# Queries split in two halves, and score buffers handed back by their readers' own signals, in the sparse attention of a decoder step

## The reference

```
o_c, p_c = _sdpa(qb, kc, vc, dist_c, dist_c >= 0, slopes_a)      # 32 compressed keys
...
o_s, _ = _sdpa(qb[:, :, None], kg, vg, dist_s, dist_s >= 0, slopes_a)   # selected blocks: all 16 of 16 here
...
o_w = _window_banded(qn, kw[:, w_buf:], vw[:, w_buf:], slopes_a)        # the last 512 keys
...
o_a = g[..., 0, :] * o_cs[..., 0, :] + g[..., 1, :] * o_cs[..., 1, :] + g[..., 2, :] * o_w
```

## Time and profile before

| | |
|---|---|
| device time, median of 3 runs | 2226.22 us (2226.08 to 2226.61) |
| the profiled execution: its time, its span | 2227.57 us, 2225.8 us |
| mean granted TensorE clock | 0.955 |
| the sparse attention | 715.8 to 1024.0 us of the span |
| TensorE busy in it | 287.48 us of 308.20 us |
| VectorE, ScalarE busy in it | 216.52 us, 177.07 us |
| ScalarE's operations for `qhi` in it | 8 of 1.02 us |
| VectorE's subtractions for `qlo` in it | 8 of 1.23 us |

### The profile page before, as it was taken

How to read it: one execution, slowest core, us unless ns; L and a number is a source line. 1 busy time by engine, 2 the same in 40 slices (tenths; PEclk the granted TensorE clock), 3 DMA queues, 4 the chain that set the end, 5 groups by cost and what they waited for, 6 DMA issues and landing times. The chain is left out here.

```text
span 2225.8 us, 34082 instructions
## 1 busy us (share of the span) xinstructions
PE 2040.4 (92%) x12618; PEld 1822.0 (82%) x12618; DVE 1140.2 (51%) x2499; ACT 621.7 (28%) x1204; POOL 114.6 (5%) x174
## 2 busy tenths in 40 slices
PE   6989999998995999998888969699999999999997
PEld 1338889878995888887667957499999999999996
DVE  0434333332234677776786644455555555555555
ACT  2113333321223565655771012211101111111012
POOL 1021100001300000000120000000000000000000
PEclk9989998999996999998998989899999999999998
DMA  9765544321101000000003431221111111101104
GB/s 318 259 190 177 158 142 147 107 79 49 49 1 62 1 2 1 1 1 1 1 0 117 148 141 40 67 79 36 57 37 48 57 28 57 57 28 57 38 0 153
DMA packets 132539, 166.42 MB, mean 75 GB/s; under 512 B 15852, under 2 KB 98636, under 8 KB 132373
## 3 DMA queue, kind: packets, MB, share of 16 engines
q1 hardware_dynamic: 117790, 134.75, 19.0%
q0 software_dynamic: 4832, 17.15, 2.4%
q10 hardware_dynamic: 9808, 13.11, 1.7%
HBM read 144.31 MB, written 22.77 MB: 75 GB/s over the span
## 5 line engine op out<-in xcount | busy, mean ns | idle before, releaser
L1673 DVE TENSOR_TENSOR late_x<-late_x,ffn_po 128x344 f32<-128x344 f32 x528 | 244.3, 509 | 116.3 <-PE ffn_po L1603 116.1
L1586 PE MATMUL ffn_pg<-late_words_hi,ffn_uhi 128*128 128x344 f32 x528 | 169.3, 321 | 14.8 <-DVE ffn_ulo L1637 14.8
L1547 ACT ACTIVATE ffn_sg<-ffn_pg 128x344 f32<-128x344 f32 x66 | 30.2, 458 | 534.2 <-PE ffn_pg L1586 534.2
L1603 PE MATMUL ffn_po<-ffn_a_hi,ffn_ohi 128*128 128x344 f32 x528 | 169.0, 320 | 0.2 <-DVE late_x L1673 0.2
L1586 PE MATMUL ffn_pg<-late_words_lo,ffn_uhi 128*128 128x344 f32 x528 | 169.1, 320 | 0.0
L1586 PE MATMUL ffn_pg<-late_words_hi,ffn_ulo 128*128 128x344 f32 x528 | 169.1, 320 | 0.0
L1603 PE MATMUL ffn_po<-ffn_a_hi,ffn_olo 128*128 128x344 f32 x528 | 168.9, 320 | 0.0
L1586 PE MATMUL ffn_pv<-late_words_hi,ffn_uhi 128*128 128x344 f32 x528 | 168.8, 320 | 0.0
L1586 PE MATMUL ffn_pv<-late_words_lo,ffn_uhi 128*128 128x344 f32 x528 | 168.7, 319 | 0.0
L1586 PE MATMUL ffn_pv<-late_words_hi,ffn_ulo 128*128 128x344 f32 x528 | 168.7, 319 | 0.0
L1603 PE MATMUL ffn_po<-ffn_a_lo,ffn_ohi 128*128 128x344 f32 x528 | 168.2, 319 | 0.0
(11 more groups left out here) (465 smaller groups left out, 4654.0 us busy)
## 6 DMA issues: line engine op xcount, KB each, us to landing
mod_wr<-in_w_ada SPq DMA_DIRECT2D x12, 2048.0 KB, 8.8
ffn_raw_u<-in_w_ffn_in SPq DMA_DIRECT2D x44, 512.0 KB, 5.8
kin_kin<-in_cache_kv SPq DMA_DIRECT2D x64, 256.0 KB, 3.5
ffn_raw_o<-in_w_ffn_out SPq DMA_DIRECT2D x22, 512.0 KB, 3.5
gate_d<-dec_gate ACTq DMA_DIRECT2D x48, 172.0 KB, 2.9
late_x<-gate_d SPq DMA_DIRECT2D x8, 1032.0 KB, 5.3
dec_raw<-in_w_in POOLq DMA_DIRECT2D x16, 512.0 KB, 5.6
dec_vin<-in_cache_kv SPq DMA_DIRECT2D x64, 128.0 KB, 2.1
```

Source lines behind the costliest of these rows:

```text
L1547: act.activation(sg[(j + c) % 2][:], pg[(j + c) % 2][:, 0:TCH], ACT.Silu).then_inc(silu_done, 1)
L1586: mm = pe.matmul(bank[b][:, 0:TCH], w[j][:, v * KD + k, :], h[:, k, tok], start=(k == 0 and q == 0), stop=(k == KD - 1 and q == 2))
L1603: mm = pe.matmul(po[u % 4][:, 0:TCH], w[j][:, k * P:(k + 1) * P], a[j][:, tok], start=(q == 0), stop=(q == 2))
L1673: dve.tensor_tensor(total[:, k, tok], total[:, k, tok], po[u % 4][:, 0:TCH], ALU.add).then_inc(o_read, 1)
```

## The change

First, ScalarE and VectorE treat the queries in two halves of 512 columns each: `qhi` is made by two operations, each with an increment of `q_hi`, and `qlo` by two, each of which waits for its half. The second operation on VectorE may begin when the second on ScalarE is done. TensorE needs both halves (`q_lo`, new) before it scores with them or overwrites the buffer.

Second, `sc_free` goes. TensorE waits, by the kind of item n - 2 (the new function `drained`), for the semaphore which the operation that reads that buffer increments itself: `q_lo`, `c_in` (new), `c_ev`, `c_add` or `biased`. With it VectorE's wait for its own operation and the separate increment go, 144 times in all: 16 units, "turned" and "blocks" in each of 8 heads. One wait is new on VectorE: `biased`, ahead of the operations that halve the slope tables at the start of heads 1 to 7.

```diff
--- before.py
+++ after.py
@@ -615,8 +615,8 @@
         if at == Q_AT and h + 1 < NH:
             items.append(("queries", h + 1))
         items.append(("unit", u))
-    place = {x: n for n, x in enumerate(items)}
     scored = np.cumsum([kind != "queries" for kind, x in items]).tolist()
+    HALF = SEQ // 2
     groups = [(x[5] - x[4] + 511) // 512 for x in units]
     turned_up_to = np.cumsum([0] + groups).tolist()
     second = np.cumsum([0] + [n - 1 for n in groups]).tolist()
@@ -638,7 +638,7 @@
         tp = [s.ps(f"tp{i}", [P, 512]) for i in range(2)]
         out = [s.ps(f"out{i}", [P, 2, P]) for i in range(2)]
         q_dup, q_ps, q_hi = s.sem("q_dup"), s.sem("q_ps"), s.sem("q_hi")
-        sc_full, sc_free = s.sem("sc_full"), s.sem("sc_free")
+        sc_full, q_lo, c_in = s.sem("sc_full"), s.sem("q_lo"), s.sem("c_in")
         tab, biased, p_full = s.sem("tab"), s.sem("biased"), s.sem("p_full")
         tp_full, tp_act, tp_dve = s.sem("tp_full"), s.sem("tp_act"), s.sem("tp_dve")
         pv_done, o_free, shares, o_step = s.sem("pv_done"), s.sem("o_free"), s.sem("shares"), s.sem("o_step")
@@ -699,17 +699,30 @@
                                            g.z[:, k0 // P + q, VCOL[b]:VCOL[b] + P], start=(q == 0), stop=(q == nt - 1))
                     mm.then_inc(pv_done, 1)
 
+                def drained(kind, x):
+
+                    if kind == "queries":
+                        pe.wait_ge(q_lo, 2 * x + 2)
+                    if kind == "compressed":
+                        pe.wait_ge(c_in, x + 1)
+                    if kind == "turned":
+                        pe.wait_ge(c_ev, x + 1)
+                    if kind == "blocks":
+                        pe.wait_ge(c_add, x + 1)
+                    if kind == "unit":
+                        pe.wait_ge(biased, x + 1)
+
                 for n, (kind, x) in enumerate(items):
                     slot = n % 2
                     if n >= 2:
-                        pe.wait_ge(sc_free, n - 1)
+                        drained(*items[n - 2])
                     if kind == "queries":
                         pe.wait_ge(q_dup, 2 * x + 2)
                         for t in range(TT):
                             mm = pe.transpose(sc[slot][:, t * P:(t + 1) * P], qd[:, t].rearrange("p a b -> p (a b)"), g.ident[:])
                         mm.then_inc(q_ps, 1)
                     if kind == "compressed":
-                        pe.wait_ge(sc_free, place["queries", x] + 1)
+                        pe.wait_ge(q_lo, 2 * x + 2)
                         for i in range(TT):
                             mm = score(slot, 32 * i, x, i, 0, 32, g.kkc)
                         mm.then_inc(sc_full, 1)
@@ -752,7 +765,8 @@
                 for n, (kind, x) in enumerate(items):
                     if kind == "queries":
                         act.wait_ge(q_ps, x + 1)
-                        act.activation(qhi[x % 2][:], sc[n % 2][:], ACT.Copy).then_inc(q_hi, 1)
+                        for a in range(0, SEQ, HALF):
+                            act.activation(qhi[x % 2][:, a:a + HALF], sc[n % 2][:, a:a + HALF], ACT.Copy).then_inc(q_hi, 1)
                     if kind == "unit":
                         h, k, i, b, k0, k1 = units[x]
                         if x >= LAG:
@@ -821,27 +835,27 @@
                 for n, (kind, x) in enumerate(items):
                     at_sc = sc[n % 2]
                     if kind == "queries":
-                        dve.wait_ge(q_hi, x + 1)
-                        dve.tensor_tensor(qlo[x % 2][:], at_sc[:], f32(qhi[x % 2][:]), ALU.subtract).then_inc(sc_free, 1)
+                        for y, a in enumerate(range(0, SEQ, HALF)):
+                            dve.wait_ge(q_hi, 2 * x + y + 1)
+                            dve.tensor_tensor(qlo[x % 2][:, a:a + HALF], at_sc[:, a:a + HALF], f32(qhi[x % 2][:, a:a + HALF]),
+                                              ALU.subtract).then_inc(q_lo, 1)
                     if kind == "compressed":
+                        if x:
+                            dve.wait_ge(biased, x * NU)
                         for t in (g.tcmp, g.tsel, g.twin):
                             halve_slopes(t)
                         dve.wait_ge(tab, x * 3 + 3)
                         dve.wait_ge(sc_full, scored[n])
                         tn = lambda a: a.rearrange("p (t n) -> p t n", t=TT)
-                        dve.tensor_tensor(scmp[:], tn(at_sc[:, 0:TT * 32]), tn(g.tcmp[:]), ALU.add).then_inc(sc_free, 1)
-                        dve.wait_ge(sc_free, n + 1)
+                        dve.tensor_tensor(scmp[:], tn(at_sc[:, 0:TT * 32]), tn(g.tcmp[:]), ALU.add).then_inc(c_in, 1)
+                        dve.wait_ge(c_in, x + 1)
                     if kind == "turned":
                         dve.wait_ge(sc_full, scored[n])
                         dve.tensor_copy(pcT[:].rearrange("p a b -> p (a b)"), at_sc[:, 0:2 * P]).then_inc(c_ev, 1)
-                        dve.wait_ge(c_ev, x + 1)
-                        dve.sem_inc(sc_free, 1)
                     if kind == "blocks":
                         dve.wait_ge(sc_full, scored[n])
                         dve.tensor_copy(g.z[:, 0:TT, C_QN + x * HD:C_QN + (x + 1) * HD],
                                         at_sc[:, 0:TT * HD].rearrange("p (t d) -> p t d", d=HD)).then_inc(c_add, 1)
-                        dve.wait_ge(c_add, x + 1)
-                        dve.sem_inc(sc_free, 1)
                     if kind == "unit":
                         h, k, i, b, k0, k1 = units[x]
                         w = SEQ if b == 0 else WINDOW + P
@@ -851,8 +865,6 @@
                             dve.wait_ge(tp_full, turned_up_to[x - 3])
                         dve.tensor_tensor_reduce(prob[x % 4][:, 0:k1 - k0], at_sc[:, 0:k1 - k0], table[:, w - (k1 - k0):w], -1.0, 3e38,
                                                  ALU.add, ALU.min, nmax[:, x % NU:x % NU + 1]).then_inc(biased, 1)
-                        dve.wait_ge(biased, x + 1)
-                        dve.sem_inc(sc_free, 1)
                         compressed(h, x % NU)
                         if x >= LAG and groups[x - LAG] == 2:
                             second_half(x - LAG)
```

## The result

The changed kernel took 2211.57 us (2210.30 to 2214.97, 4 runs) against 2226.41 (2226.08 to 2226.85, 4 runs): ratio 0.9936, 95% interval 0.9918 to 0.9953, 14.8 us less. Timed once more beside before (e7_again) it was 13.7 us less.

The account below looks back on a forecast made before the run. The prediction took TensorE to bound the sparse attention, busy 287.48 of 308.20 us. Terms 2.5 + 2.9 + 2.3 + 0.6 - 0.1 = 8.2 us off 2226.22 gave 2218.0 us, range 2213.5 to 2222.9.

Parts of the forecast that it names:

- unit 4's term: At a head's start, TensorE's 0.22 us stand before unit 4's scores, for unit 3's accumulator read and increment, is all won.
- the term of head 0: In head 0, where TensorE starts at half clock, the same savings of 0.96 us give 0.6, bounds 0.4 and 1.0.
- Nothing else of the later stages changes: Behind the sparse attention, apart from one more semaphore clear, the stages only begin earlier; 2 us each way allowed for clock.
- The queries: At unit 11's scores, halving `qhi` and `qlo` shortens TensorE's wait by 0.36 us, seven times: 2.5 us.
- The gap behind a unit: On VectorE after each unit's accumulator read, dropping wait and increment saves 0.20 us, between 0.10 and 0.23.
- The start of a head: TensorE gains 0.20 us at the copy behind unit 1 and 0.22 at unit 4, 0.42 a head: 2.9 us.
- Behind "blocks": VectorE begins unit 5 0.29 us earlier after its copy of the blocks, shortening a TensorE stall; eight heads: 2.3 us.
- It is the bound, and all that can be won here is the 20.7 us in which it stands: In the sparse attention TensorE, busy 287.48 of 308.20 us, can gain only its idle time, located by the table of waits.
- my rival of the clock that gives more: Head 0's half-clock stretch of 6.5 us vanishes as TensorE's pauses shrink: 11.4 us won, 2214.8; chance 0.13.
- The one semaphore more: GpSimd clears one more semaphore at the stage's end while TensorE waits: at most 0.09 us, 0.1 taken off.
- The upper bound of my sum: The gain over the whole kernel with every term at its high bound, given as 9.8 us.

Follow-up runs that it names:

- e10: The changed kernel with VectorE's wait for itself and a separate increment put back behind the copy of "blocks" alone, once in each head: 2215.25 us.
- e6: The changed kernel with VectorE's wait for itself, without increment, put back behind the first four units of head 0 alone: 2215.62 us.
- e11: The changed kernel with the queries whole and placed ahead of unit 12 instead of unit 10: 2206.69 us, ratio to before 0.9920.
- e8: The changed kernel with the item queries placed ahead of unit 12 instead of unit 10, still in halves: 2202.24 us, ratio to before 0.9889.

## Why the prediction was right, and where it was wrong

The mechanisms of the sum were right and the sum was too small. The stage became 12.3 us shorter, where my terms for it add up to 8.3; the steps that failed are the reading of the listed waits as all stalls, the size of unit 4's term, and the term of head 0. With the stage's 12.3 alone the median would be 2214.1, inside the range. What put it below is 2.5 us more outside the stage, where I had "Nothing else of the later stages changes"; its cause stays open.

**The queries** (2.5 us): right. 0.36 each, and the rows fit the working to 0.01.

**The gap behind a unit** (0.20): right in mechanism; measured 0.22 (from 0.14 behind the read to 0.08 ahead of its end), and 0.29 where the copy follows. The Trainium skill ("VectorE: DVE Perf Modes", "The DRAIN you can't avoid") says that one can't skip the pause between VectorE operations by chaining them without semaphores, and that the semaphore costs nothing extra. For waits on the engine's own result the rows here show otherwise: the same copy begins 0.21 behind the read, 0.04 behind it or with it, by what VectorE's sequencer has to do in between.

**The start of a head** (0.42): 0.53. Mis-sized was the 0.22 at unit 4, 0.30 measured: I took the pace of TensorE's transposes for the time it needs before the scores; the weight load's row had 0.29.

**Behind "blocks"** (0.29): right, 0.31; e10 shows the cause to be the one that I read, not the row's releaser.

**"It is the bound, and all that can be won here is the 20.7 us in which it stands"** failed, with the table of waits as the list of stalls. The 0.13 is a stall inside a row of five transposes: in the merged row they last 0.86 before and 0.73 after, and no wait of TensorE's is listed for them in a steady head. It comes seven times, 0.9 us. Together, a steady head won 1.35 where I had 1.07.

**Head 0** (0.6) failed most. With its "blocks" it had 0.9 in my sum, and won 2.29. Of this, some 1.5 is the slow stretch that halved: e6, e10 and the pair e11 and e8 put the price of the longer one at 1.4 to 1.6. The rest, 0.8, is about the 0.9 that I had forecast. So my rival of the clock that gives more came true in part. I priced it as another case, with 0.13, instead of asking how near it was, and in another execution of the same kernel (e10 up to there) it did not come.

The account of the stage: heads 1 to 6 together won 8.7 from one mark to the next where I had 6.4 (six times 0.28 more, and 0.6 that single heads of before had lost more, most of it in head 1 at the same unlisted stall), head 0 2.3 for 0.9, the end 1.4 for 1.1. The one semaphore more took 0.08, of the 0.1 allowed. The upper bound of my sum should read 9.7, not 9.8.

**Outside the stage** 1.4 to 2.5 us more went in the two timings of the changed kernel. Median less stage is 1919.2, 1918.7, 1919.6 and 1917.1 in four groups of before; 1916.7 and 1918.1 for the changed kernel; 1914.3 to 1920.6 over the experiments. Kernels whose stage was shortened by 2.6 or by 21 us show no order in it. Between the two profiled executions, 2227.57 and 2214.97 us, the difference is 12.6, of which the stage has 12.3. Single runs scatter by 3 to 6 us within a kernel, and already the start of this stage, ahead of which all kernels are the same, lay between 711.1 and 715.9 us in the fourteen profiles. So I count the 2.5 as scatter of single runs; that isn't shown, and whether later stages gain a little by beginning earlier stays open.

## What to carry to other kernels

Release a buffer by the increment of the operation that reads it: a wait for the engine's own result with a separate increment holds up the engine's next operation too (here by 0.22 to 0.29 us), and that is felt two engines further on. Where a later operation of the same engine overwrites what this one reads, the wait stays, but ahead of that operation, as `biased` ahead of the slope tables here. Before an operation on the path is split, look whether the item can stand where the waiting engine has more work: one number in a hand-written order won as much in a steady head as both edits, and left the split 0.08 us of its 0.36 there. Count stalls from the starts of matmuls, and from the weight loads, not from the matmuls' waits alone.

## What the runs showed of the hardware

In this stage VectorE's next operation starts with the accumulator read (0.08 us ahead of its end) when its queue holds no wait for the read itself, also with one or two other waits in between that are already met; 0.04 us behind its end with a wait for that read; 0.14 behind with a separate increment as well; and 0.21 when two more waits follow that increment. And TensorE's slow stretch in head 0 (granted 0.50) was 3.4 us long or twice that; between the changed kernel and e10 the stretch began only 0.15 us apart against the same work.
